# A fifth pair of hidden units with seven block products in each layer, and another order of the block sums

## What is computed

```python
def swiglu(h, w_gate, w_up, w_down):
    return (jax.nn.silu(h @ w_gate) * (h @ w_up)) @ w_down

for layer in range(DEPTH):
    ...
    h = rms_norm(x, ffn_norm[layer])
    x = x + swiglu(h, ffn_w_gate[layer], ffn_w_up[layer], ffn_w_down[layer])
return rms_norm(x, final_norm)
```

## Time and profile before

| | us |
|---|---|
| median of 3 runs | 1937.71 (1937.54 to 1938.13) |
| time of the profiled execution | 1938.14 |
| its span, first to last instruction | 1936.4 |
| PE busy | 1924.4 (99%) |
| DVE busy | 1396.6 (72%) |
| ACT busy | 925.2 (48%) |

### The profile page before, as it was taken

How to read it: one execution, slowest core, us unless ns; L and a number is a source line. 1 busy time by engine, 2 the same in 40 slices (tenths; PEclk the granted TensorE clock), 3 DMA queues, 4 the chain that set the end, 5 groups by cost and what they waited for, 6 DMA issues and landing times.

```text
span 1936.4 us, 21975 instructions
## 1 busy us (share of the span) xinstructions
PE 1924.4 (99%) x9268; PEld 1611.4 (83%) x9268; DVE 1396.6 (72%) x1044; ACT 925.2 (48%) x723; POOL 23.7 (1%) x85
## 2 busy tenths in 40 slices
PE   9999999999999999999999999999999999999998
PEld 7889999988888888888888887788888888888886
DVE  6656788855757868878779556756877868968755
ACT  6444334436434545545445345633544544645443
POOL 1000000000000000000000030000000000000000
PEclk9999999999999999999999999999999999999999
DMA  9555444455555654747666655464575765746762
GB/s 307 178 177 165 153 152 152 149 178 164 183 196 190 244 196 174 276 139 251 242 207 227 223 183 167 137 209 152 205 273 175 254 203 194 260 133 238 260 210 94
DMA packets 214874, 380.92 MB, mean 197 GB/s; under 512 B 5937, under 2 KB 55170, under 8 KB 214530
## 3 DMA queue, kind: packets, MB, share of 16 engines
q1 hardware_dynamic: 214560, 379.10, 57.3%
q10 hardware_dynamic: 226, 0.55, 0.1%
HBM read 377.53 MB, written 2.10 MB: 196 GB/s over the span
## 4 chain that ended last, share of the span: by engine, by line
PE 90%; DVE 8%; ACT 1%; issue 0%; DMA 0%; SPq 0%; ACTq 0%
PE main L1595 39%; PE main L1601 19%; PE main L1537 8%; PE aux L1617 5%; PE main L1539 4%; DVE lo L990 4%; DVE raw L996 4%; PE aux L1621 3%; PE main L1617 2%; PE aux L1544 2%; PE main L1621 2%; PE aux L1706 1%; ACT hi L634 1%; PE main L1648 1%; PE main L1650 1%; PE main L1649 1%
## 5 line engine op out<-in xcount | busy, mean ns | idle before, releaser
L634 ACT CAST hi<-raw 128x2048 fp32r<-128x2048 f32 (+1 forms) x389 | 742.5, 1909 | 778.6 <-PE main L1601 492.9
L990 DVE TENSOR_TENSOR lo<-raw,hi 128x2048 fp32r<-128x2048 f32 x316 | 719.6, 2290 | 322.2 <-ACT hi L634 322.2
L1595 PE MATMUL main<-hi,act 128*128 128x512 f32 x1968 | 470.0, 391 | 0.0
L1595 PEld LDWEIGHTS main<-hi,act 128*128 128x128 f32 x1968 | 368.1, 188 | 77.5 <-issue 1.9
L1595 PE MATMUL main<-hi,mid 128*128 128x512 f32 x1616 | 385.6, 391 | 0.0
L1595 PEld LDWEIGHTS main<-hi,mid 128*128 128x128 f32 x1616 | 301.7, 188 | 63.0 <-DVE mid L1257 0.5
L1601 PE MATMUL main<-lo,act 128*128 128x512 f32 x984 | 243.1, 389 | 0.0
L1537 PE MATMUL main<-act,hi 128*128 128x512 f32 x640 | 229.1, 401 | 0.0
L981 DVE TENSOR_TENSOR lo<-raw,hi 128x2048 fp32r<-128x2048 f32 x71 | 162.6, 2290 | 80.0 <-ACT hi L634 80.0
L1601 PEld LDWEIGHTS main<-lo,act 128*128 128x128 f32 x984 | 184.7, 188 | 38.3
L1601 PE MATMUL main<-lo,mid 128*128 128x512 f32 x808 | 199.6, 389 | 0.0
(11 more groups left out here) (180 smaller groups left out, 1329.9 us busy)
## 6 DMA issues: line engine op xcount, KB each, us to landing
raw<-in_ffn_w_gate SPq DMA_DIRECT2D x104, 1024.0 KB, 5.3
raw<-in_ffn_w_up SPq DMA_DIRECT2D x88, 1024.0 KB, 6.4
raw<-in_ffn_w_down SPq DMA_DIRECT2D x88, 1024.0 KB, 5.0
raw<-in_ab_w_in SPq DMA_DIRECT2D x55, 1024.0 KB, 5.1
raw<-in_ab_w_out SPq DMA_DIRECT2D x16, 1024.0 KB, 5.0
raw<-in_pool_w SPq DMA_DIRECT2D x4, 1024.0 KB, 5.5
xn<-in_x SPq DMA_DIRECT2D x4, 512.0 KB, 8.3
raw<-in_ab_w_in SPq DMA_DIRECT2D x2, 512.0 KB, 6.5
```

Of the source, the lines that this page charges most:

```text
L634: return nc.scalar.copy(out_, in_)
L990: V.tensor_tensor(lo[:, split_at(t), :], src, hi[:, split_at(t), :].bitcast(F32), ALU.subtract).then_inc(lo_ready, 1)
L1595: mm(o2[:, h, :], lhs[:, k0 + n, c, h * P:(h + 1) * P], w_hi, start=(first and c == 0 and n == 0), stop=False)
```

## The change

Each layer now has one plain unit and five pairs. `UNITS` becomes (3, 2, 2, 2, 2), where the 3 is a plain unit and a pair. The plain unit's gate and up come first (8 slots), then at once block 0 of the first pair. The plain unit's hidden tile is transposed in the middle of that block, into `bank_b` in place of `aux`, and its down projection (four slots, `g.early`, into alternating banks) stands between the first pair's x slots and its second up. The gate results of that pair are put together (`combine`) while the early slots run. The last group of a layer is an ordinary pair; what was attached to its twelve down slots (turning x for the next layer, the final gain) is attached to slots 4, 5 and 6 of eight.

In all pairs the block sums are made in another order. Before: behind the `lo` of slot k of a block two sums, behind k+1 one, behind k+2 one. Now: one before the `lo` of slot k, none behind it, one behind k+1, two behind k+2. The four sums are the same four tensors; b12+b22 is now got by subtracting b11 from the threefold sum.

```diff
-UNITS = (2, 2, 2, 2, 3)
+UNITS = (3, 2, 2, 2, 2)
...
-FFN_SLOTS = 12 * UNIT_ALL + 6 * (len(UNITS) - 1)
-FFN_JOBS = 2 * UNIT_ALL + 4 * len(UNITS) - 3 * (len(UNITS) - 1)
+FFN_SLOTS = 12 * UNIT_ALL + 6 * len(UNITS)
+FFN_JOBS = 6 + 5 * len(UNITS)
...
+PAIR_DOWN = ((0, 0), (1, 0), (0, 1), (1, 1), (2, 0), (2, 1), (3, 0), (3, 1))
+AFTER = {4: 0, 5: 1, 6: 2}
...
+        g = Group(layer, u + n - 2, len(UNITS) * layer + index)
+        if g.first:
+            g.slot, g.job = s, j
+            s, j = s + 8, j + 6
+        g.blocks, g.x = (s, s + BLOCK + 4), s + 2 * BLOCK + 4
+        up_a, s = s + BLOCK, g.x + 2
+        if g.first:
+            g.early = tuple(range(s, s + 4))
+            s += 4
+        g.ups, g.j_up = (up_a, s), j
+        s, j = s + 4, j + 1
+        g.down, g.j_down = tuple((s + k, m, i) for k, (m, i) in enumerate(PAIR_DOWN)), j
+        s, j, u = s + 8, j + 4, u + n
...
-            free += [(b22.at, s + 3), (b11.at, s + 4), (b12.at, s + 5), (b21.at, s + 6)]
+            free += [(b22.at, s + 3), (b12.at, s + 4), (b11.at, s + 5), (b21.at, s + 6)]
...
-SOURCE = (0, 0, 2, 0, 1, 3)
+SOURCE = (0, 1, 2, 1, 0, 3)
...
-SUM_FOR = {1: 1, 3: 3, 4: 2, 5: 4}
+SUM_FOR = {1: 1, 3: 2, 4: 3, 5: 4}
...
+                    for m, s in enumerate(g.early):
+                        place(PLACES[s][0], wide_rows(w_down[layer], WIDE * (g.a - 1), WIDE * m))
+                    unit(w_up[layer], g.ups[1], g.a + 1)
...
             def prepare(t):
 
-                ve.wait_ge(hi_ready, t + 1)
                 s0, i = BLOCK_OF.get(t, (t, 0))
                 at = [p.at for p in PLACES[s0]]
-                src = raw[:, at[SOURCE[i]], :]
-                V.tensor_tensor(lo[:, split_at(t), :], src, hi[:, split_at(t), :].bitcast(F32), ALU.subtract
-                                ).then_inc(lo_ready, 1)
-                if t not in BLOCK_OF:
-                    return
-
-                def add(a, b):
-                    V.tensor_tensor(raw[:, at[a], :], raw[:, at[a], :], raw[:, at[b], :], ALU.add
-                                    ).then_inc(sum_made, 1)
+
+                def add(a, b, op=ALU.add):
+                    V.tensor_tensor(raw[:, at[a], :], raw[:, at[b], :], raw[:, at[a], :], op).then_inc(sum_made, 1)
 
                 def loaded(n):
                     ve.wait_ge(raw_loaded[at[n]], 16 * PLACES[s0][n].lap)
 
-                if i == 0:
+                if t in BLOCK_OF and i == 0:
+                    loaded(0)
                     loaded(1)
-                    add(0, 1)
+                    add(1, 0)
+                ve.wait_ge(hi_ready, t + 1)
+                V.tensor_tensor(lo[:, split_at(t), :], raw[:, at[SOURCE[i]], :], hi[:, split_at(t), :].bitcast(F32),
+                                ALU.subtract).then_inc(lo_ready, 1)
+                if t in BLOCK_OF and i == 1:
                     loaded(2)
                     add(1, 2)
-                if i == 1:
-                    add(0, 2)
-                if i == 2:
+                if t in BLOCK_OF and i == 2:
+                    ve.wait_ge(sum_made, BLOCK_SUMS * block_index(s0) + 2)
+                    add(0, 1, ALU.subtract)
                     loaded(3)
-                    ve.wait_ge(sum_made, BLOCK_SUMS * block_index(s0) + 3)
-                    add(3, 0)
+                    add(3, 1)
...
+                    for m, s in enumerate(g.early):
+                        combine(g, m)
+                        add_residual(Count(s), (bank_a, bank_b)[(m + 1) % 2], m)
+                        prepare(s + AHEAD)
+                    for b in range(4):
+                        s = g.ups[1] + b
+                        if not g.first:
+                            combine(g, b)
+                        if b == 3:
+                            ve.wait_ge(sig_used, 3 * g.pair + 3)
+                            up_out(s, 1, norm)
+                        prepare(s + AHEAD)
+                        if b == 2:
...
+                if k == 0 and g.first:
+                    pe.wait_ge(job_emptied, g.job + 2)
+                    turn_hidden(g.layer, g.a - 1, 1, bank_b)
...
+                    if g.first:
+                        pe.wait_ge(turn_taken, T_HIDDEN[layer] + 1)
...
+                    for m, s in enumerate(g.early):
+                        if m == 1:
+                            pe.wait_ge(gate_ready, 4 * g.pair + 2)
+                        if m > 1:
+                            pe.wait_ge(job_emptied, g.job + m + 1)
+                        wide(s, (bank_a, bank_b)[(m + 1) % 2], mid, 0, True, True)
...
+                    pe.wait_ge(job_emptied, g.j_up - 1 if g.first else g.j_up)
+                    for b in range(4):
+                        wide(g.ups[1] + b, bank_b, act, 4 * b, b == 0, b == 3)
+                        if b == 2:
+                            pe.wait_ge(sig_used, 3 * g.pair + 2)
```

More of the change, by code:

```diff
@@ L88 @@
     layer: int
-    unit: int
-    n: int
-    pair: int = 0
+    a: int
+    pair: int
     blocks: tuple = ()
@@ L95 @@
     j_up: int = 0
-    plain: tuple = ()
+    slot: int = 0
+    job: int = 0
+    early: tuple = ()
     down: tuple = ()
@@ L906, in _ @@
+                for g in groups:
+                    if g.first:
+                        for b in range(8):
+                            s = g.slot + b
                             if b == 3:
-                                keep_up(s, g, norm)
+                                sc.wait_ge(row_rstd, 2 * layer + 2)
+                                sc.wait_ge(a_ready, 2 * layer + 1)
+                                unit_out(s, bank_a, norm, 3 * g.pair)
                             prepare(s + AHEAD)
-                        for i in range(BLOCK):
-                            s = g.blocks[1] + i
-                            if i == 0:
-                                sc.wait_ge(slot_used, s + 1)
-                                copy(c11, bank_x).then_inc(p1_kept, 1)
-                            prepare(s + AHEAD)
@@ L932, in _ @@
[L932 to L944 removed]
+                            start_of_layer(layer, b)
@@ new lines, in _ @@
+                    for i in range(BLOCK):
+                        prepare(g.blocks[0] + i + AHEAD)
+                        if g.first and i == 2:
+                            take_hidden(layer, g.a - 1, 0, bank_b)
+                    for b in range(4):
+                        s = g.ups[0] + b
+                        if b == 3:
+                            keep_up(s, g, norm)
+                        prepare(s + AHEAD)
+                    for i in range(BLOCK):
+                        s = g.blocks[1] + i
+                        if i == 0:
+                            sc.wait_ge(slot_used, s + 1)
+                            copy(c11, bank_x).then_inc(p1_kept, 1)
+                        prepare(s + AHEAD)
@@ L1466, in _ @@
+                for g in groups:
+                    e = g_of[:, 1, 1, :]
+                    if g.first:
+                        for b in range(8):
+                            s = g.slot + b
                             if b == 3:
-                                ve.wait_ge(sig_used, 3 * g.pair + 3)
+                                ve.wait_ge(row_rstd, norm + 1)
+                                gate_out(layer, g.a - 1, 1, norm, T_HIDDEN[layer])
+                            if b == 7:
+                                ve.wait_ge(job_emptied, g.job + 1)
@@ new lines, in _ @@
+                    for i in range(BLOCK):
+                        prepare(g.blocks[0] + i + AHEAD)
+                        if g.first and i == 2:
+                            take_hidden(layer, g.a - 1, 0, bank_b)
+                    for b in range(4):
+                        prepare(g.ups[0] + b + AHEAD)
+                    for i in range(BLOCK):
+                        prepare(g.blocks[1] + i + AHEAD)
+                    prepare(g.x + AHEAD)
+                    ve.wait_ge(p1_kept, g.pair + 1)
@@ L1488, in _ @@
+                    for b in range(4):
+                        s = g.ups[1] + b
+                        if not g.first:
+                            combine(g, b)
+                        if b == 3:
+                            ve.wait_ge(sig_used, 3 * g.pair + 3)
+                            up_out(s, 1, norm)
+                        prepare(s + AHEAD)
+                        if b == 2:
+                            take_hidden(layer, g.a, 0)
                     for n, (s, m, i) in enumerate(g.down):
-                        if i == g.n - 1 and s + 1 < SLOTS:
+                        if i == 1 and s + 1 < SLOTS:
@@ new lines, in _ @@
+                    need(pe, gates_out, g.pair)
+                    pe.wait_ge(a_ready, 2 * layer + 1)
+                    gate_block(g, 0)
+                    if g.first:
+                        pe.wait_ge(turn_taken, T_HIDDEN[layer] + 1)
+                    else:
+                        pe.wait_ge(job_emptied, g.j_up)
+                    for b in range(4):
```

(4 more changed lines are left out.)

307 lines of the change are left out of this document (116 added, 191 removed).

## The result

The changed kernel took 1983.15 us in the median of six runs (1979.56 to 1985.41), the kernel before 1937.92 us (1937.54 to 1939.21): 2.3% slower, ratio 1.0229 with a 95% interval of 1.0219 to 1.0239. The forecast was 1969.6 us, range 1960 to 1976. The direction was right, the time is outside the range, 13.6 us above the forecast. The profiled execution took 1980.5 us.

The account below looks back on a forecast made before the run. PE was taken to bound the kernel, busy 1924.4 of 1936.4 us. Terms -10.9 + 8.2 + 17.6 + 4.6 + 4.6 + 7.8 = +31.9 us gave a span of 1968.3 and a time of 1969.6 us, range 1960 to 1976.

Parts of the forecast that it names:

- The bound: Whole kernel: PE busy for 1924.4 of 1936.4 us, so time is PE's instructions plus its waits.
- the removed matmuls: Gate of two units per layer: 24 matmuls or 5.44 us less a layer, -10.9 us in all.
- First blocks of the old pairs: Block 0 of eight pairs: PE waits 1.02 us longer for the fourth product's `lo`, +8.2 us in all.
- Second blocks: Second block of eight old pairs: two sums delay the fourth product's `lo` by 2.20 us, +17.6 us in all.
- New first blocks: First block of each layer's new pair: PE waits 2.1 us in layer 0, 2.5 in layer 1, +4.6 us.
- New second blocks: Second block of the two new pairs: 2.29 us each from no wait before, +4.6 us.
- Early slots: Second early down slot in each layer: PE waits 3.9 us for DVE to read bank_a, +7.8 us.
- the rival that named it: Clock halves in new waits: 1973 us if in the two 3.9 us waits (10%), 2007 us if in all 22 (1%).
- cover: All blocks: sum 1 uses idle time, `lo` k+3 comes no later, kernel faster at 1924 to 1929 us; 4%.
- cheaper first pair: New pairs: early wait at its lower end, no wait in new first blocks, 1960 us; 10%.
- more waits: New first pair: a `lo` behind block 0 also late by two sums (4.4 us) per layer, 1978 us; 7%.
- The signs: New profile: 20 PE waits for `lo`, two of 3.9 us, 48 PE instructions and 10.9 us busy time fewer, DVE +71 us.

Follow-up runs that it names:

- the kernel with both causes taken away: Changed kernel with old sum order, DVE's last bank_a reads earlier, activations' sums for k = 1 in the first pair's block 0: 1927.08 us, ratio 0.9942.
- second trace of the changed kernel: Changed kernel run and profiled once more, nothing edited: 1984.55 us, trace span 1982.8 us.
- the 1.9 us kernel: Kernel before plus two unused DVE reductions over 885 columns behind every block's fourth sum, 16 PE waits of 1.88 and 2.04 us: 1982.48 us, ratio 1.0225.

## Why the prediction was wrong, point by point

**The bound, and the removed matmuls.** Right: -10.9 us, as the kernel with both causes taken away shows (-11.1 in the span).

**First blocks of the old pairs, +1.02 each.** Measured +1.02, and the forecast start of `lo` k+3 relative to the block (612.95 - 604.06 = 8.89 us) is 683.27 - 674.37 = 8.90 in the new trace. **Second blocks, +2.20 each.** Measured +2.19, with DVE's 2.04 us of idle time in front of `lo` k+2. **New first blocks, 2.1 and 2.5.** Measured 1.80 and 2.23 idle, 2.0 and 2.4 late. **New second blocks, 2.29.** Measured 2.28.

**Early slots, 3.9 each.** 4.0 us late in layer 0 (583.38 + 1.81 = 585.19 to 589.19), 3.0 in layer 1. The mechanism was right; what differs is when the loads of the three `lo` in front landed. In the second trace of the changed kernel the two were 4.21 and 2.08 us of idle time, so this term lies between 2 and 4 us by execution. I had taken one value for both layers.

Together the delays are 8.2 + 17.5 + 4.4 + 4.6 + 7.0 = 41.7 us against 42.8 in the forecast. This part of the working needs no correction.

**The step that failed: no term for the clock.** The sum had none, and the rival that named it came in two forms, both wrong: only the two early waits (10%), or all 22 (1%). The case between, some of the waits of 2 us, was not there, and it is the one that holds. Of the profiled execution's excess over the forecast (1978.8 - 1968.3 = 10.5 us) the clock is 9.7, the waits -1.1, and 1.9 us are left that I can't place. The runs' median is 2.7 us above the profiled execution, which one or two losses more would make; the mean granted clock points the same way (0.994 in the fastest of the six runs, 0.989 in the slowest). The price of a single loss was right: 1.7 us, drawn from the earlier trace rows. That it fits is in part luck: the forecast took it from a stretch of 3.47 us at the kernel's start without a reason why a fall in mid-kernel should last as long, and it had no double losses. What was wrong is the chance. The trace of before had no idle time of PE between 0.5 us and the stretch at the start, so no row there could tell whether 1 or 2 or 4 us suffice. I put 10% on something that the trace was silent about, when every new wait in the sum was a case for it. An honest bracket would have been 0 to 1.7 us for each of the 14 waits of 2 us and more that the sum itself had: 1970 to 1993 us, which holds the result.

**Rivals 1, 2 and 4** (cover, cheaper first pair, more waits) didn't occur. The last is refuted by the count of 20 waits.

**The signs.** All that the forecast named were there: 20 waits of 1.3 and 2.3 us by the delay, DVE's idle time of about 2 us, two early waits, 48 instructions fewer, DVE at +78.9 us (forecast at least 71). The one that failed is PE's busy time: 10.9 us less was forecast, 2.6 more was measured. The clock's losses stand in it, since slow matmuls count as busy.

## What to carry to other kernels

Where PE bounds a kernel and runs at full clock, a new wait of about 2 us or more can cost more than its length. As the table above has it for these kernels: 1.7 us more for about half of those between 1.9 and 2.7 us, for nearly all from 3 us on (some double, 2.6 to 3.1 us), and nothing up to 1.8 us. Give the range both ends, and expect the kernel's runs to scatter more than before. Before moving work on a helper engine, write down its queue around the operand that the bounding engine needs last: work put into idle time ahead gains nothing if the next thing in the queue waits for another engine, and then all that is put behind it is paid in full. A saving on the bounding engine comes through entirely once its new waits are gone: the fifth pair was worth 10.9 us all along, and the new order of the sums, the early slots and the opening sums had hidden it.

## What the hardware showed that I had not expected

- Behind 2 us of idle time the granted clock fell in about half of the cases (35 of 64 waits from 1.87 to 2.24 us) and in none of 65 up to 1.8 us. A fall cost 1.7 us (clock 0.66 over 5 us), a double one 2.6 to 3.1 us (0.74 to 0.78 over 12 us), part of its low clock lying in the idle time in front.
- Which waits are hit differs from one execution to the next, but waits at equal distances were sometimes hit in rows (four in a row in both traces of the 1.9 us kernel). Longer waits aren't always hit more often: five of 16 at 2.5 to 2.7 us against 16 of 32 at 1.9 to 2.0. Whether that is chance or comes from the distances of these kernels' pairs stays open.
- The times scatter more with it: six runs of the changed kernel span 5.9 us, five of the kernel without such waits 1.0 us (1926.92 to 1927.91). It is a hint only, since the kernel before, with no such wait either, spans up to 2.9 us in three runs (1937.69 to 1940.54).
- Eight matmuls that nothing uses, put into each of the ten idle times of the second blocks, kept the clock up and made a kernel 6.9 us faster.
- Two DVE operations of which the second reads the first's result took 0.12 us more than two independent ones (4.61 against 4.49 us).
